# Reordering the second block of a two-block transformer kernel: tables, remainders, scores, maxima and turns

## What is computed

```python
def second_block(x, p, norm_mix_g, w_in, ...):
    h = rmsnorm(x, norm_mix_g[i])
    z = h @ w_in[i]
    qa, ka, va, qb, kb, vb, ga, gb = jnp.split(z, split_at, axis=-1)
    y_a = mixer_a(qa, ka, va, q_norm_g[i], k_norm_g[i], row_ids, col_ids) @ w_out_a[i]
    y_b = mixer_b(qb, kb, vb, rel_bias) @ w_out_b[i]
    gate_a = jax.nn.sigmoid(ga + b_gate[i, :D_MODEL])
    gate_b = jax.nn.sigmoid(gb + b_gate[i, D_MODEL:])
    x = x + (gate_a * y_a + gate_b * y_b) @ w_out[i]
    h = rmsnorm(x, norm_mlp_g[i])
    x = x + jnp.square(jax.nn.relu(h @ w_ff1[i])) @ w_ff2[i]
    ...

def mixer_a(q, k, v, q_g, k_g, row_ids, col_ids):
    q = axial_rope(rmsnorm(q, q_g), row_ids, col_ids) * (hd ** -0.5)   # 8 heads of 128
    k = axial_rope(rmsnorm(k, k_g), row_ids, col_ids)                  # 2 heads
    ...  softmax(q k^T) v over all 256 tokens
```

## Time and profile before

| | us |
|---|---|
| median of 3 runs | 1044.67 (1044.17 to 1048.76) |
| the profiled execution | 1044.55 |
| its span, first to last instruction | 1042.9 |
| PE busy | 999.4 (96%) |
| PE weight loads busy | 822.3 (79%) |
| DVE busy | 695.8 (67%) |
| ACT busy | 517.5 (50%) |
| mean rate of the transfers | 209 GB/s |

### The profile page before, as it was taken

How to read it: one execution, slowest core, us unless ns; L and a number is a source line. 1 busy time by engine, 2 the same in 40 slices (tenths; PEclk the granted TensorE clock), 3 DMA queues, 4 the chain that set the end, 5 groups by cost and what they waited for, 6 DMA issues and landing times.

```text
span 1042.9 us, 13046 instructions
## 1 busy us (share of the span) xinstructions
PE 999.4 (96%) x4742; PEld 822.3 (79%) x4742; DVE 695.8 (67%) x1072; ACT 517.5 (50%) x651; POOL 44.3 (4%) x82
## 2 busy tenths in 40 slices
PE   7999999989999898999999999899999999999996
PEld 5878888868877776888888878788887888888875
DVE  6968777878996786755444887345566764545557
ACT  5563433484764547434433554554463644344354
POOL 0001111100000000000000020002000000000000
PEclk9999999999999999999999999999999999999999
DMA  9976988837755354965555466314334565454531
GB/s 375 415 259 243 361 306 332 285 105 266 289 221 198 104 202 159 334 238 194 198 174 190 186 227 242 122 69 133 133 116 170 184 237 197 167 201 163 199 121 41
DMA packets 37040, 217.81 MB, mean 209 GB/s; under 512 B 4448, under 2 KB 5216, under 8 KB 16006
## 3 DMA queue, kind: packets, MB, share of 16 engines
q1 hardware_dynamic: 26604, 179.66, 47.0%
q0 software_dynamic: 9104, 34.08, 9.2%
q10 hardware_dynamic: 1290, 3.50, 1.0%
HBM read 216.16 MB, written 3.69 MB: 211 GB/s over the span
## 4 chain that ended last, share of the span: by engine, by line
PE 73%; DVE 15%; ACT 5%; DMA 3%; issue 2%; DVEq 0%; ACTq 0%; POOLq 0%; SPq 0%
PE YP L450 10%; PE YP L452 10%; PE YP L451 10%; PE GP L450 10%; PE GP L452 10%; PE GP L451 10%; DVE wlo L1703 6%; DMA raw<-in_stream 2%; ACT whi L1164 2%; DVE arena L1859 1%; PE TP L450 1%; PE TP L452 1%; PE TP L451 1%; DMA ada<-in_ada_t 1%; DVE ada L1850 1%
## 5 line engine op out<-in xcount | busy, mean ns | idle before, releaser
L1703 DVE TENSOR_TENSOR wlo<-raw,whi 128x2048 fp32r<-128x2048 f32 x158 | 360.8, 2290 | 175.1 <-ACT whi L1164 173.8
L1164 ACT ACTIVATE whi<-raw 128x2048 fp32r<-128x2048 f32 x160 | 306.3, 1917 | 250.1 <-PE YP L452 121.4
L450 PE MATMUL GP<-whi,hT 128*128 128x512 f32 x480 | 189.8, 395 | 4.2 <-DVE wlo L1703 3.2
L452 PE MATMUL GP<-whi,hT 128*128 128x512 f32 x480 | 187.1, 390 | 0.0
L451 PE MATMUL GP<-wlo,hT 128*128 128x512 f32 x480 | 186.9, 389 | 0.0
L450 PE MATMUL YP<-whi,bT 128*128 128x512 f32 x334 | 131.7, 394 | 1.8 <-ACT arena L1218 1.0
L452 PE MATMUL YP<-whi,bT 128*128 128x512 f32 x334 | 130.2, 390 | 0.0
L451 PE MATMUL YP<-wlo,bT 128*128 128x512 f32 x334 | 130.0, 389 | 0.0
L450 PE MATMUL YP<-whi,hT 128*128 128x512 f32 (+1 forms) x288 | 117.1, 407 | 4.9 <-DVE hT L1798 2.7
L452 PE MATMUL YP<-whi,hT 128*128 128x512 f32 (+1 forms) x288 | 112.4, 390 | 0.0
L451 PE MATMUL YP<-wlo,hT 128*128 128x512 f32 (+1 forms) x288 | 112.1, 389 | 0.0
(11 more groups left out here) (334 smaller groups left out, 1135.3 us busy)
## 6 DMA issues: line engine op xcount, KB each, us to landing
raw<-in_stream SPq DMA_DIRECT2D x161, 1024.0 KB, 4.9
ada<-in_ada_t POOLq DMA_DIRECT2D x48, 512.0 KB, 5.9
arena<-in_ada_t SPq DMA_DIRECT2D x8, 1024.0 KB, 10.9
arena<-in_ada_t POOLq DMA_DIRECT2D x8, 512.0 KB, 6.1
bias_scratch<-bias_row POOLq DMA_DIRECT2D x1, 2560.0 KB, 16.1
arena<-in_b_gate ACTq DMA_DIRECT2D x2, 1024.0 KB, 7.3
ada<-bias_scratch POOLq DMA_DIRECT2D x16, 128.0 KB, 3.8
x<-in_x SPq DMA_DIRECT2D x2, 512.0 KB, 4.1
```

What stands on the lines that cost most here:

```text
L450: nc.tensor.matmul(out_ap, xT[0][:, k, tok], hi, start=start, stop=False)
L452: return nc.tensor.matmul(out_ap, xT[1][:, k, tok], hi, start=False, stop=stop)
L1164: nc.scalar.activation(whi[:, slot, :], raw[:, slot, :], ACT.Copy).then_inc(w_hi, 1)
L1703: nc.vector.tensor_tensor(wlo[:, slot, :], raw[:, slot, :], whi[:, slot, :].bitcast(F32), ALU.subtract)\
```

## The change

1. **Tables.** The 20 products become a function `axial_tables` that DVE runs inside the feed forward before, between its two loops. Their transfer is issued by ACT in the first block's mixer, behind `merged_hi(4, KD)`, and counts on the semaphore that the causal mask had.
2. **Remainders.** Unit 98's `lo` goes ahead of the rotation of the keys, and 99 ahead of the first half of the queries; 100 and 101 follow, then 102. Unit 106 goes behind the first two maxima, 107 behind the first `out_a`. ACT's rounding of 107 goes behind the first exponentials.
3. **Turns and scores.** Turn 4 follows turn 3 ahead of the chunk; turns 5 and 6 follow it; then come the scores of heads 0 and 1, and turns 7 to 10 stand behind chunks 0 to 3. ACT's copies 8 and 9 are between `exps_a(0)` and `exps_a(1)`, copy 10 behind. 
4. **Maxima.** DVE takes the maximum of head or step n + 2 before `gate_in` and the scaling of n. The small buffers for maxima and denominators are used in rotation of four, not two, and `exps_a` no longer waits for `oa_set`.
5. **Merged turns.** Turning the first half of `merged2` stands ahead of the last chunk of `U_WOA + 2`, the second half ahead of k = 3 of `U_WO2`.
6. **End.** The last residual sum goes ahead of the `lo` of `U_FF + 1`.

The work itself stays the same. The diff, cut:

```diff
@@ PE
+            for r in range(4):
+                turn_z(r)
+                if r == 3:
+                    turn_z(4)
+                chunk_of(U_ZB + 4, 4 + r)
+            turn_z(5)
+            turn_z(6)
+            pe.wait_ge(sig("aT_copied"), 5)
+            scores_a(0)
+            scores_a(1)
+            for r in range(7, 11):
+                more_chunks(r - 7, r - 6)
+                turn_z(r)
...
             for h in range(HA):
                 more_chunks(*BEFORE_A[h])
+                if h == 0:
+                    pe.wait_ge(sig("aT_copied"), 11)
                 mix_a(h)
...
-            project(U_WOA + 2, oaT, KD, T01)
+            for k in range(KD):
+                if k % 4 == 0:
+                    pe.wait_ge(w_lo, U_WOA + 3 + k // 4)
+                if k == KD - 1:
+                    merged2_turn(0)
...
+            for k in range(KD):
+                if k % 4 == 0:
+                    pe.wait_ge(w_lo, U_WO2 + k // 4 + 1)
+                if k == 3:
+                    merged2_turn(1)
+                pe.wait_ge(sig("mT2"), k + 1)
@@ ACT
             merged_hi(4, KD)
+            act.dma_start(tabs_a[:, 0:2, :, :], A["axial"]).then_inc(sig("table_loaded"), 16)
...
-            act.dma_start(tabs_a[:, 0:2, :, :], A["axial"]).then_inc(sig("b_gate"), 16)
...
-            a_copy(4)
+            a_copy(5)
+            a_copy(6)
             his(106, 107)
-            for r in range(5, 11):
-                a_copy(r)
-            his(107, 108)
+            a_copy(7)
...
                 if h >= 2:
                     act.wait_ge(sig("pa_turned"), h - 1)
-                    act.wait_ge(sig("oa_set"), h - 1)
...
             exps_a(0)
+            a_copy(8)
+            a_copy(9)
+            exps_a(1)
+            a_copy(10)
             for h in range(HA):
-                if h + 1 < HA:
+                if h == 0:
+                    his(107, 108)
+                elif h + 1 < HA:
                     exps_a(h + 1)
@@ DVE
                     with dve.Fori(1, 3) as i:
                         group(i, True)
+                    axial_tables()
                     with dve.Fori(3, GROUPS - 1) as i:
                         group(i, False)
...
+            los(u + 3, u + 4)
             rotate(zkv[:, :, 0:HKV * DA], HKV, 1)
-            los(u + 3, u + 4)
+            los(u + 4, u + 5)
             rotate_q(0)
-            los(u + 4, u + 6)
+            los(u + 5, u + 7)
             rotate_q(1)
-            los(u + 6, u + 8)
+            los(u + 7, u + 8)
...
             for h in range(HA):
-                if h == HA - 1:
-                    gate_in(0)
-                out_a(h)
                 if h + 2 < HA:
                     max_a(h + 2)
                 else:
                     max_b(h + 2 - HA)
+                if h == HA - 1:
+                    gate_in(0)
+                out_a(h)
+                if h == 0:
+                    los(u + 12, u + 13)
...
             for s in range(HB * T):
+                if s + 2 < HB * T:
+                    max_b(s + 2)
                 if s in (2, 5):
                     gate_in((2, 5).index(s) + 1)
                 out_b(s)
-                if s + 2 < HB * T:
-                    max_b(s + 2)
...
+            residual(4, 1, 1, U_WO2 + 4, gtbank, None)
             los(U_FF + 1, U_FF + 2)
-            residual(4, 1, 1, U_WO2 + 4, gtbank, None)
```

More of the change, by code:

```diff
@@ L941, in _, with scores_a, turn_z @@
             pe.wait_ge(sig("rot_a"), 3)
-            for r in range(11):
+            def scores_a(h):
+                if h >= 2:
+                    pe.wait_ge(sig("pa_ready"), h - 1)
+                for t in range(T):
+                    last = nc.tensor.matmul(GP[:, (h % 2) * N + t * S:(h % 2) * N + (t + 1) * S],
+                                            QaT[:, h, t * P:(t + 1) * P], KaT[:, h // 4, :],
+                                            start=True, stop=True)
+                last.then_inc(sig("sa_ready"), 1)
+            def turn_z(r):
                 if r >= 2:
@@ L954, in _ @@
                 last.then_inc(sig("a_turned"), 1)
-                if r < 4:
-                    chunk_of(U_ZB + 4, 4 + r)
-                elif r in (6, 7, 8, 9):
-                    more_chunks(r - 6, r - 5)
-            pe.wait_ge(sig("aT_copied"), 11)
-            pe.wait_ge(sig("z_copied"), 5)
-            def scores_a(h):
-                if h >= 2:
-                    pe.wait_ge(sig("pa_ready"), h - 1)
-                for t in range(T):
-                    last = nc.tensor.matmul(GP[:, (h % 2) * N + t * S:(h % 2) * N + (t + 1) * S],
-                                            QaT[:, h, t * P:(t + 1) * P], KaT[:, h // 4, :],
-                                            start=True, stop=True)
-                last.then_inc(sig("sa_ready"), 1)
+            for r in range(4):
[11 more added lines that the diff above has]
+                turn_z(r)
             def mix_a(h):
@@ L1079, in _, with merged2_turn @@
             project(U_WOA, oaT, KD, G01, N, ("oaT", 0))
-            project(U_WOA + 2, oaT, KD, T01)
-            for half in range(2):
+            def merged2_turn(half):
                 pe.wait_ge(sig("merged2"), half + 1)
@@ L1088, in _ @@
                         last.then_inc(sig("m2_turned"), 1)
-                for k in range(4 * half, 4 * half + 4):
-                    if k % 4 == 0:
-                        pe.wait_ge(w_lo, U_WO2 + half + 1)
-                    pe.wait_ge(sig("mT2"), k + 1)
-                    for t in range(T):
-                        last = passes(bank(GP, t), mT2, k, t, (U_WO2 + half) % SLOTS, k % 4 * N, N,
-                                      k == 0, k == KD - 1)
-                last.then_inc(w_used, 1)
+            for k in range(KD):
[3 more added lines that the diff above has]
+                    merged2_turn(0)
+                for t in range(T):
+                    last = passes(bank(TP, t), oaT, k, t, (U_WOA + 2 + k // 4) % SLOTS, k % 4 * N, N, k == 0, k == KD - 1)
+                if k % 4 == 3:
+                    last.then_inc(w_used, 1)
+            for k in range(KD):
[4 more added lines that the diff above has]
+                pe.wait_ge(sig("mT2"), k + 1)
+                for t in range(T):
+                    last = passes(bank(GP, t), mT2, k, t, (U_WO2 + k // 4) % SLOTS, k % 4 * N, N, k == 0, k == KD - 1)
+                if k % 4 == 3:
+                    last.then_inc(w_used, 1)
             project_tiles(U_WO2 + 2, mT2, KD, T01, 4, 4)
@@ L1538, in _ @@
                 if n == 2:
-                    for r in range(4):
+                    for r in range(5):
                         a_copy(r)
@@ L1893, in rope_tables, with axial_tables @@
                                 .then_inc(sig("tables"), 1)
+            def axial_tables():
+                dve.wait_ge(sig("table_loaded"), 32)
+                cosx, sinx = tabs_a[:, 0], tabs_a[:, 1]
+                for w, name in ((1, "ka"), (0, "qa")):
+                    g = row(name)
+                    for t in range(T):
+                        for half in range(4):
+                            a = slice(32 * half, 32 * half + 32)
+                            o = 32 * (half ^ 1)
+                            nc.vector.tensor_tensor(tabs_a[:, 2 * w + 1, t, a], g[:, o:o + 32], sinx[:, t, a], ALU.mult)
+                        ins = nc.vector.tensor_tensor(tabs_a[:, 2 * w, t, :], g[:, :], cosx[:, t, :], ALU.mult)
+                    link(ins)
             def swiglu(f, u0):
@@ L2158, in masked_max @@
                 if h == 0:
[L2159 removed]
+                    dve.wait_ge(sig("table_loaded"), 16)
                 if h >= 2:
@@ L2343, in _ @@
             link(nc.vector.tensor_scalar(rs[:, 0:16], rs[:, 0:16], A_SCALE, None, ALU.mult))
-            los(u + 8, u + 10)
-            los(u + 10, u + 13)
-            dve.wait_ge(sig("b_gate"), 48)
+            los(u + 8, u + 11)
+            dve.wait_ge(sig("b_gate"), 32)
             def gate_in(n):
```

29 lines of the change are left out of this document (8 added, 21 removed).

## The result

| | before | after |
|---|---|---|
| median of 4 runs, us | 1045.12 (1044.17 to 1048.76) | 1033.27 (1032.86 to 1034.65) |
| ratio, 95% interval | | 0.988 (0.986 to 0.991) |
| span of the profiled execution | 1042.9 | 1031.7 |

The account below looks back on a forecast made before the run. PE was taken as the bound, busy for 999.4 of 1042.9 us, with gains only in its waits: 3.56 + 4.80 + 2.04 + 0.60 = 11.0 us, so 1044.67 - 11.0 = 1033.7 us. The range was 1032.0 to 1037.5 us.

Parts of the forecast that it names:

- Rival 2: Units 98 to 102: late weight transfers keep half of each of two waits, 1.8 us lost, 1035.5 us; chance 7%.
- rival 1: Turns and first exponentials: PE waits for ACT's fuller queue, the 4.80 us is not gained, 1038.5 us; chance 14%.
- rival 3: First exponentials: copies at four more borders switch ACT's function set, 1.28 us per load, 1037 to 1038.8 us; chance 1%.
- 0.15 us late: First feed forward: 2.68 us of tables against 2.53 of DVE idle time delay group 3's first `lo` by 0.15, costing nothing.
- no later than before: Sign in the first feed forward: group 3's first `lo` comes no later than before, and PE does not wait.
- Gain 0, cost 0: Mixers: taking maxima ahead of scaling only fills DVE's idle time before `gate_in`, so it is worth 0 us.
- the 0.90 at head 1's copy: Mixer A: PE's wait for head 1's copy of turned probabilities, 0.90 us, goes, counted within the turns' 4.80.
- Rival 4: Mixers: early maxima block DVE when bias tiles come late; 1049.7 us at 4 us for each tile; chance 2%.
- PE turns at 823.13 without a wait: 0.6 us: Start of the second feed forward: the last residual sum, placed ahead of a `lo`, removes PE's wait, 0.6 us.
- no bracket DVE wlo on PE between the two feed forwards: Sign on PE's timeline: between the feed forwards no wait for a DVE remainder is shown any more.
- bracket + 0.16: All PE stalls: each costs its shown wait plus 0.16 us, the tail of a matmul otherwise overlapped.
- the lower end: Range's fast limit, 1032.0 us: all waits, 11.4, `gate_in`'s 0.38, and 1.3 for slower passes behind waits and scatter.

Follow-up runs that it names:

- tables_times3: The changed kernel with the keys' half of the tables formed five times instead of once, so the tables take three times as long: 1034.76 us.
- undo_maxima: The changed kernel with the maxima behind `gate_in` and the scaling again, as before the change: 1034.07 us.
- ff_lo_first: The changed kernel with the `lo` of `U_FF + 2` between the second feed forward's two norm factors instead of behind both: 1032.41 us.

## Why the prediction was right, and where it was not

| stretch | predicted | measured |
|---|---|---|
| tables in the feed forward (A) | 0 | 0.00 |
| remainders (B) | 3.56 | 3.85 |
| turns, scores, exponentials, maxima (C) | 4.80 | 5.22 |
| merged turns (D) | 2.04 | 2.23 |
| residual (E) | 0.60 | 0.08 |
| sum | 11.0 | 11.38 |

**The remainders.** Right in kind and place. The `lo`s of 98, 99, 100 and 102 were replayed to end at 614.2, 619.0, 626.8 and 636.8; DVE's timeline of after, which runs 0.2 us later as a whole, has (each ends 2.2 us behind its start, so at 613.8, 618.7, 626.5 and 636.5; a row with x2 holds two)

```profile
611.63 2.29 DVE L1729 TENSOR_TENSOR wlo<-raw,whi 128x2048 fp32r<-128x2048 f32 x1
...
616.49 2.29 DVE L1729 TENSOR_TENSOR wlo<-raw,whi 128x2048 fp32r<-128x2048 f32 x1
...
624.27 4.49 DVE L1729 TENSOR_TENSOR wlo<-raw,whi 128x2048 fp32r<-128x2048 f32 x2
...
634.25 2.29 DVE L1729 TENSOR_TENSOR wlo<-raw,whi 128x2048 fp32r<-128x2048 f32 x1
```

Rival 2, the transfers, did not come. ACT's rounding of unit 101, which had waited 3.92 us for its transfer, now waits for PE:

```profile
623.26 1.92 ACT L1186 ACTIVATE whi<-raw 128x2048 fp32r<-128x2048 f32 x1 [1.28 <-PE GP L452]
```

**Turns and first exponentials.** The replay of ACT's list (table load until 659.0, copies 8 and 9 until 661.3, copy 10 until 663.2) stands in after's timeline almost to the tenth, so rival 1 did not come either:

```profile
657.80 1.28 ACT L1576 ACT_TABLE_LOAD   x1
659.09 0.56 ACT L1576 ACTIVATE arena<-GP,nm,rs 128x256 f32<-128x256 f32 x1
...
660.19 1.27 ACT L1555 ACTIVATE arena<-TP 128x512 f32<-128x512 f32 x2
661.36 0.56 ACT L1576 ACTIVATE arena<-GP,nm,rs 128x256 f32<-128x256 f32 x1
...
662.71 0.60 ACT L1555 ACTIVATE arena<-TP 128x512 f32<-128x512 f32 x1
```

The function table is loaded once here, as before, and seven times in the whole program, as before: the copies between the exponentials cause no other load, and rival 3 falls. (Its four more borders between exponentials and copies were miscounted: by ACT's lists there are two more.)

**Tables.** Right that they cost nothing, but not by the argument given. The first `lo` of group 3 was to be 0.15 us late. It starts 9.65 us behind the landmark (449.70 against 440.05) where it had started 9.11 behind it, so it is 0.54 late: DVE stands still for 0.2 us on either side of the tables, and the replay had put that at nothing. The sign "no later than before" was not met, yet PE did not notice, and `tables_times3` shows what would have bound it first, the hidden rows.

**Maxima.** "Gain 0, cost 0" was wrong, and hidden by its neighbour. I had looked for PE's waits in heads 2 to 7 and found none, and had counted the 0.90 at head 1's copy to the turns. That wait hangs on a maximum (head 2's) that has to be ahead of a scaling: `undo_maxima` costs 1.04. The sum was right because the term was counted, under the wrong edit; that is luck. Rival 4, the bias tiles, did not come: stretch C shows no other wait.

**The residual.** The step that failed is "PE turns at 823.13 without a wait: 0.6 us", which is true of the turn and stops there. It did not ask what is late next. The next thing was the `lo` of `U_FF + 2` behind two norm factors, on a chain that comes only 0.08 us earlier when PE arrives 0.6 earlier. Before the change its lateness was covered, but for 0.12 us, by the very stall that was removed. So the prediction's sign "no bracket DVE wlo on PE between the two feed forwards" held, but a bracket of 0.53 came behind them, and PE's idle time fell by 8.5 us, not 9.4.

**The size of a stall.** The price of bracket + 0.16 came out low by about 0.1 in all other terms: 3.85 - 3.56 for two stalls, 2.23 - 2.04 for two, 5.22 - 4.80 for five. In B and D that is the pass behind a wait, which the earlier trace rows shows busy for 0.50 (0.47 in the earlier trace rows) and not 0.39; I had named it for the lower end and left it out of the sum. In C other instructions stand behind the waits, and what makes up the 0.42 there was not taken apart. At 0.1 more for each the ten stalls make 12.0 us, and with the residual at its measured 0.08 they make 11.4, the measured sum. It also fits PE's busy time, said to be unchanged: it fell by 2.7 us, of which nine stalls fewer make 2.4, at 0.16 each (the tail shown alone instead of overlapped) and 0.11. So it is in part luck that the forecast came within 0.4 us of 11.38: a term 0.5 too high met others 0.9 too low.

## To carry to other kernels

When a stall is taken out of the engine that bounds the kernel, follow that engine on to its next operand and ask what that operand's chain starts from; if it doesn't start at the stall, the gain may end there. Price parts that stand close together by replaying the lists of the waited-for engines, one part at a time, since a wait can belong to an edit that looks idle. And compare two kernels by the distances between landmarks of the bounding engine: here they repeat within 0.07 us, where the runs of most kernels scatter by 1 us and more.

## What the runs showed of the hardware

A stall costs PE more than its bracket: 0.16 us of tail that is shown as busy and would have been overlapped, and about 0.1 in the pass behind it (0.50 busy and 0.34 to the next start, as at 821.37, instead of 0.39 and 0.23). A stall of up to 0.15 us had no bracket at all, and showed only as a distance of 0.37 between starts and a first pass of 0.50 (`ff_lo_first`, 820.22 to 820.59). Copies between exponentials on ACT loaded no function table again; the one load took 1.28 us, and the exponential behind it started 1.29 us after the load (657.80 to 659.09).
